# Hybrid encoder trunk on one core: every second expert-up tile as 512-column matmuls, and 112 of 256 router candidates

## What is computed

```python
def peer_ffn(h, w_query, q_norm_peer, sub_keys_1, sub_keys_2, expert_u, expert_v):
    s1, s2 = ...                      # 8 heads, 128 scores each, per token
    v1, i1 = lax.top_k(s1, 16)
    v2, i2 = lax.top_k(s2, 16)
    cand_s = v1[..., :, None] + v2[..., None, :]          # 16 x 16 = 256 sums
    cand_i = i1[..., :, None] * 128 + i2[..., None, :]
    top_s, top_pos = lax.top_k(cand_s, 16)                # of 256
    idx = jnp.take_along_axis(cand_i, top_pos, axis=-1)
    g = jax.nn.softmax(top_s, axis=-1)
    ...
    act = gelu(u[idx] . h)            # u: 16384 x 1024
    y = sum(g * act * v[idx])         # v: 16384 x 1024
```

## Time and profile before

| | us |
|---|---|
| median of three runs | 2226.91 (2225.76 to 2228.22) |
| the profiled execution, its own time | 2227.43 |
| its span, first to last instruction | 2225.6 |
| TensorE busy | 2164.8 (97%) |
| VectorE busy | 1656.9 (74%) |
| ScalarE busy | 1217.0 (55%) |

### The profile page before, as it was taken

How to read it: one execution, slowest core, us unless ns; L and a number is a source line. 1 busy time by engine, 2 the same in 40 slices (tenths; PEclk the granted TensorE clock), 3 DMA queues, 4 the chain that set the end, 5 groups by cost and what they waited for, 6 DMA issues and landing times.

```text
span 2225.6 us, 45150 instructions
## 1 busy us (share of the span) xinstructions
PE 2164.8 (97%) x14996; PEld 1996.6 (90%) x14996; DVE 1656.9 (74%) x3155; ACT 1217.0 (55%) x2134; POOL 268.7 (12%) x298
## 2 busy tenths in 40 slices
PE   4999999999999999999989999999999999999998
PEld 4889989999999988888878899899999999888887
DVE  6787766889589956777557868588895998567765
ACT  3656555444577654545455565644445776454544
POOL 0210000000157500000002100000001772000000
PEclk7999999999999999999999999999999999999999
DMA  8566655555533357787545666455555334588765
GB/s 321 169 209 216 209 171 169 180 180 178 185 127 114 114 195 255 253 257 229 196 174 171 224 213 214 138 182 183 180 184 174 114 113 135 195 274 256 254 214 162
DMA packets 114452, 427.48 MB, mean 192 GB/s; under 512 B 12704, under 2 KB 12960, under 8 KB 113056
## 3 DMA queue, kind: packets, MB, share of 16 engines
q1 hardware_dynamic: 114336, 426.08, 57.3%
HBM read 424.98 MB, written 1.05 MB: 191 GB/s over the span
## 4 chain that ended last, share of the span: by engine, by line
PE 94%; DVE 2%; issue 1%; DMA 1%; ACT 1%; POOL 0%; SPq 0%; ACTq 0%; DVEq 0%; POOLq 0%
PE pj L1290 18%; PE pj L1291 17%; PE pj L1292 17%; PE wk L1290 10%; PE wk L1292 10%; PE wk L1291 10%; PE wk L1602 5%; DMA arena<-in_front 1%; PE wk L1402 1%; PE wk L1379 1%; PE wk L1341 1%; PE wk L1395 1%; PE wk L1542 0%; PE wk L1315 0%; PE wk L1424 0%
## 5 line engine op out<-in xcount | busy, mean ns | idle before, releaser
L797 DVE TENSOR_TENSOR lo<-raw,hi 128x1024 fp32r<-128x1024 f32 x683 | 840.3, 1232 | 475.8 <-ACT hi L471 468.0
L471 ACT ACTIVATE hi<-raw 128x1024 fp32r<-128x1024 f32 x683 | 721.6, 1057 | 468.6 <-PE wk L1292 345.1
L1290 PE MATMUL pj<-mov_hi,hi 128*128 128x256 f32 x3248 | 945.5, 291 | 31.6 <-DVE mov_lo L848 27.5
L1291 PE MATMUL pj<-mov_lo,hi 128*128 128x256 f32 x3248 | 921.3, 284 | 0.0
L1292 PE MATMUL pj<-mov_hi,lo 128*128 128x256 f32 x3248 | 921.2, 284 | 0.0
L1290 PEld LDWEIGHTS pj<-mov_hi,hi 128*128 128x128 f32 x3248 | 624.2, 192 | 47.1 <-DVE mov_lo L848 30.4
L1291 PEld LDWEIGHTS pj<-mov_lo,hi 128*128 128x128 f32 x3248 | 625.9, 193 | 0.2
L1292 PEld LDWEIGHTS pj<-mov_hi,lo 128*128 128x128 f32 x3248 | 624.9, 192 | 0.0
L1290 PE MATMUL wk<-hi,mov_hi 128*128 128x512 f32 x1024 | 398.6, 389 | 1.7 <-DVE mov_lo L1239 1.7
L1292 PE MATMUL wk<-hi,mov_lo 128*128 128x512 f32 x1024 | 398.4, 389 | 0.0
L1291 PE MATMUL wk<-lo,mov_hi 128*128 128x512 f32 x1024 | 398.4, 389 | 0.0
(11 more groups left out here) (184 smaller groups left out, 1507.9 us busy)
## 6 DMA issues: line engine op xcount, KB each, us to landing
raw<-in_stream SPq DMA_DIRECT2D x684, 512.0 KB, 3.3
arena<-in_ada SPq DMA_DIRECT2D x72, 512.0 KB, 4.8
onehot_a<-in_ada SPq DMA_DIRECT2D x24, 512.0 KB, 4.6
arena<-in_front SPq DMA_DIRECT2D x4, 2048.0 KB, 19.3
arena<-in_taba SPq DMA_DIRECT2D x2, 1536.0 KB, 19.4
arena<-in_keys SPq DMA_DIRECT2D x2, 1024.0 KB, 6.3
x<-in_xT SPq DMA_DIRECT2D x1, 1024.0 KB, 5.0
arena<-in_mix SPq DMA_DIRECT2D x2, 512.0 KB, 16.1
```

What stands on the lines that cost most here:

```text
L471: nc.scalar.activation(hi[j % SPLIT][:, :], raw[j % RAW][:, :], ACT.Copy).then_inc(hi_done, 1)
L797: nc.vector.tensor_tensor(lo[j % SPLIT][:, :], raw[j % RAW][:, :], hi[j % SPLIT][:, :].bitcast(f32), ALU.subtract).then_inc(lo_done, 1)
L1290: pe.matmul(out, w_h, m_h, start=first, stop=False)
L1291: pe.matmul(out, w_h, m_l, start=False, stop=False)
```

## The change

**TensorE.** `mov_hi` and `mov_lo` of the first 8 chunks become one tensor `mov`, in which the high and the low part of a chunk lie side by side as 512 columns. The even ones of the 96 early up tiles use `project_half`: for each chunk one matmul of `hi` with all 512 columns (hi*hi in the left half of the bank, hi*lo in the right), and one of `lo` with the 256 high ones into the left half. The odd ones, the mixed tiles and all else go as before.

**ScalarE and VectorE.** For an even tile j, ScalarE copies the left half to `arena` (`early_half`), VectorE adds the right half to it (`second_half`, which frees the bank), and ScalarE takes the Gelu of it in place, before it evicts tile j+1. The adding of tile j stands in VectorE's order ahead of the `lo` of tile j+4, number j+1.

**The router.** `cand` has 112 places instead of 256: 4 times 16 (first half's places 0 to 3) and 12 times 4; the 16 largest sums of two sorted lists are always among these. Forming them takes two instructions, and each `max`, `match_replace` and `max_index` on it reads 112 values. The decode has five instructions more, with one `lo` subtraction more within it.

```diff
+CAND = 4 * 16 + 12 * 4
...
-        mov_hi = sb("mov_hi", [P, 12, SEQ], f32r)
-        mov_lo = sb("mov_lo", [P, 12, SEQ], f32r)
+        mov = sb("mov", [P, KC, 2, SEQ], f32r)
+        w_hi = sb("w_hi", [P, 4, SEQ], f32r)
+        w_lo = sb("w_lo", [P, 4, SEQ], f32r)
...
-        cand = part(256)
-        candr = part(256)
+        cand = part(CAND)
+        candr = part(CAND)
...
-                    act.wait_ge(tile_done, t + 1 + SPLIT)
-                    nc.scalar.activation(arena[:, bass.ds(i * 4 + j, 1), :].squeeze(1), pj[j % 2][:, 0:SEQ],
-                                         ACT.Gelu_apprx_tanh).then_inc(out_free, 1)
+                    if j % 2:
+                        wait_alone(act, out_free, l * OUTS + i * 4 + (O_PEER + j + 2))
+                        nc.scalar.activation(group(j - 1), group(j - 1), ACT.Gelu_apprx_tanh)
+                        act.wait_ge(tile_done, t + 1 + SPLIT)
+                        nc.scalar.activation(group(j), pj[1][:, 0:SEQ], ACT.Gelu_apprx_tanh).then_inc(out_free, 1)
+                    else:
+                        act.wait_ge(tile_done, t + 1 + SPLIT)
+                        nc.scalar.activation(group(j), pj[0][:, 0:SEQ], ACT.Copy).then_inc(early_half, 1)
...
+                def second_half(j):
+
+                    dve.wait_ge(early_half, l * (EARLY // 2) + j // 2 + 1)
+                    dve.wait_ge(out_free, l * OUTS + (O_PEER + j + 2))
+                    nc.vector.tensor_tensor(arena[:, j, :], arena[:, j, :], pj[0][:, SEQ:2 * SEQ], ALU.add)\
+                        .then_inc(out_free, 1)
+
                 def split_early(n):
                     for _ in range(min(n, EARLY - early[0])):
                         j = early[0]
+                        if j % 2:
+                            second_half(j - 1)
                         rest_of(L0 + (T_PEER + AHEAD + j), j + AHEAD)
                         early[0] += 1
...
-                nc.vector.tensor_scalar(pos_i[:, 0, :], tp, 4, None, ALU.logical_shift_right)
-                link(nc.vector.tensor_scalar(pos_i[:, 1, :], tp, 15, None, ALU.bitwise_and))
+                for n, (op, by) in enumerate(((ALU.logical_shift_right, 4), (ALU.logical_shift_right, 2),
+                                              (ALU.bitwise_and, 15), (ALU.bitwise_and, 12))):
+                    e = nc.vector.tensor_scalar(place_i[:, n, :], tp, by, None, op)
+                link(e)
+                split_early(1)
                 nc.vector.tensor_copy(sel_if, sel_i)
-                link(nc.vector.tensor_copy(pos_f, pos_i))
+                nc.vector.tensor_copy(place_f[:, 4, :], tp)
+                link(nc.vector.tensor_copy(place_f[:, 0:4, :], place_i))
+
+                nc.vector.scalar_tensor_tensor(pos_f[:, 0, :], place_f[:, 1, :], -12.0, place_f[:, 0, :], ALU.add, ALU.max)
+                link(nc.vector.scalar_tensor_tensor(place_f[:, 3, :], place_f[:, 4, :], 64.0, place_f[:, 3, :], ALU.is_ge,
+                                                    ALU.mult))
+                link(nc.vector.tensor_tensor(pos_f[:, 1, :], place_f[:, 2, :], place_f[:, 3, :], ALU.subtract))
                 split_early(1)
...
+                        wh, wl = chunk(j, k)
+                        both = mov[:, k, :, :].rearrange("p a s -> p (a s)")
+                        if k < KC - 1:
+                            pe.matmul(out, wh, both, start=k == 0, stop=False)
+                            pe.matmul(out[:, 0:SEQ], wl, mov_hi(k), start=False, stop=False)
+                        else:
+                            pe.matmul(out[:, 0:SEQ], wl, mov_hi(k), start=False, stop=False)
+                            last = pe.matmul(out, wh, both, start=False, stop=True)
+                    return last
```

More of the change, by code:

```diff
@@ L220, in trunk, with mov_of, mov_hi, mov_lo @@
         F_BANK = (2, 4, 3, 5)
+        def mov_of(side, k, n):
+            return mov[:, k:k + n, side, :] if k < KC else (w_hi, w_lo)[side][:, k - KC:k - KC + n, :]
+        def mov_hi(k):
+            return mov_of(0, k, 1).squeeze(1)
+        def mov_lo(k):
+            return mov_of(1, k, 1).squeeze(1)
         def y_pairs(br, i):
@@ L1329, in project, with project_half @@
                             between()
-                        last = product(pj[bank][:, 0:SEQ], *chunk(j, k), mov_hi[:, at[k], :], mov_lo[:, at[k], :],
+                        last = product(pj[bank][:, 0:SEQ], *chunk(j, k), mov_hi(at[k]), mov_lo(at[k]),
                                        k == 0, k == KC - 1)
+                    return last
+                def project_half(t, j, o, bank, chunks=None, between=None):
+                    pe.wait_ge(lo_done, t + 1)
+                    pe.wait_ge(out_free, l * OUTS + o + 1)
+                    out = pj[bank][:, :]
+                    for k in range(KC):
+                        if chunks is not None:
+                            pe.wait_ge(mov_ready, l * M_READY + (chunks + k + 1))
+                        if between is not None and k == KC // 2:
+                            between()
+                        wh, wl = chunk(j, k)
[6 more added lines that the diff above has]
+                            last = pe.matmul(out, wh, both, start=False, stop=True)
                     return last
@@ L1614, in _ @@
                                 tokens(i, j, 1)
-                            last = product(pj[j % 2][:, 0:SEQ], *chunk(j, k), mov_hi[:, k, :], mov_lo[:, k, :],
+                            last = product(pj[j % 2][:, 0:SEQ], *chunk(j, k), mov_hi(k), mov_lo(k),
                                            k == 0, k == KC - 1)
```

53 lines of the change are left out of this document (31 added, 22 removed).

## The result

The changed kernel takes **2240.23 us** (median of 4 runs, 2238.72 to 2243.03) against 2226.67 for the kernel before (median of 4): a ratio of 1.006, interval 1.0048 to 1.0073. It is 13.6 us slower. The forecast was +8.8 us with a range of 2225 to 2243: the direction and the range held, and the size fell short by 4.8 us. The profiled execution took 2240.32 us with a span of 2238.5, so between the two profiled executions the span grew by 12.9 us.

What follows compares the result with a forecast made beforehand. TensorE was taken to set the time. Picks and softmax place in two layers, less the joining gain, 2 x (7.0 + 2.5) - 10.2 = +8.8 us on 2227.43, gave 2236.2, median 2235.7 us; range 2225 to 2243.

Steps and rivals of the forecast that it cites:

- What bounds the kernel, and where: Early stage: TensorE's unbroken matmuls set the time; VectorE's additions come late in the picks and at the softmax place.
- The gain by joining: Even early tiles on TensorE: 13.3 ns saved for each of 768 joined matmuls, 10.2 us in all.
- The router: VectorE's router loop: the smaller list saves 0.86 us a round, 13.8 us a layer, none of it time gained.
- The tolerance and the picks: Additions may start 1.69 us late; VectorE's pick instructions delay tiles 62, 64, 66, 70, 74, costing 7.0 us per layer.
- The softmax place: Tile 80's addition waits behind softmax steps and a subtraction on VectorE, so tile 82 starts late: 2.5 us per layer.
- What is late next: nothing: Behind tile 82's late start nothing further is delayed: `lo` tiles are ahead and tile 84's gates are ready.
- Fewer late additions (17%): Rival, 17%: tiles 62 and 64 on time, picks stall about 4.4 us a layer: 2231, or 2227 with more lag absorbed.
- The picks without delay (10%): Rival, 10%: additions never late in the picks, only the softmax place costs: 2221.7, or 2216.7 if that is hidden.
- Stalls in the router loop (10%): Rival, 10%: slower additions (0.6 us) also stall TensorE in the router loop and lengthen picks: 2241 to 2244.
- a joined form that gains nothing (3%): Rival, 3%: a 512 behind a 256 keeps the whole cost of both, so the 10.2 us fall away: 2245.9.

Runs made afterwards that it cites:

- Removing the softmax place alone: Changed kernel with tile 80 copied and added ahead of the `lo` of tile 83 and the softmax steps: 2234.02 us, ratio 1.0029 to the kernel before.
- removing both: Changed kernel with tiles 60 to 79 multiplied and evicted as before the change, and tile 80 added ahead of the softmax steps: 2222.84 us, ratio 0.9975.
- the order by width: Changed kernel with each even tile's matmuls reordered: seven of 512 columns, eight of 256, one of 512: 2242.01 us, ratio 1.0063 to the kernel before.
- the fastest kernel: Changed kernel with tiles 60 to 79 as before, tile 80 added ahead of the softmax, joined tiles' matmuls grouped by width: 2219.54 us, ratio 0.9965.
- joining alone: Changed kernel with the old router (256 sums, old decode), keeping joined matmuls and additions: 2239.38 us, ratio 1.0052 to the kernel before.
- tiles 60 to 79 not joined: Changed kernel with tiles 60 to 79 multiplied and evicted as before the change, other even early tiles joined: 2231.81 us, ratio 1.0017 to the kernel before.
- the long late bank: Kernel before with three useless ScalarE copies at tile 80, holding its bank 2.3 us late: 2234.05 us, ratio 1.0028.
- the short late bank: Kernel before with one useless ScalarE copy at tile 80, holding its bank 1 us late: 2229.87 us, ratio 1.0011.

## Why the prediction was right in its direction and short in its size

**What bounds the kernel, and where: right.** TensorE sets the time; the stops stand where VectorE's queue is densest and at the softmax place, and nowhere else. Removing the softmax place alone gave back 6.2 to 6.9 us of 7.3 by medians and ratios, removing the picks alone 8.4 to 9.9 of 11.4, and removing both gave 17.4 of 18.7 (2240.23 to 2222.84), with no wait for an addition left.

**The gain by joining: the step that failed.** I took 13.3 ns for each joined matmul, "because both streams have a new weight load for every matmul and differ only in columns". It is 7 ns: 5.4 us instead of 10.2, and these 4.8 us are, by size, the whole error of the sum. The rates of the earlier trace rows are rates of streams of one width. In a stream that changes width twice in every chunk each change costs 2.5 ns more, as the order by width showed; that is 5 of the 6.3 ns, and the remaining 1.2 has no experiment. The prediction had noted that no row shows the two forms alternating, and should have kept the range open there instead of taking the upper end. The Trainium skill (TensorE: Matmul & The Clock Gate, Back-to-back issue gap) gives the gap of a matmul as its columns by the clock plus 2.5 ns, and gives this for an isolated one, not for a stream with a weight load before each, as this is; an estimate by that rule is 2.5 ns saved a joined pair. Measured are 7 in this order and 10.8 in the order by width (0.087 us over 8). So the rule gives too little in either order, and my 13.3 too much; the kernel as it was written lies somewhat nearer to the rule, the order by width nearer to the rates of this trace.

**The router: right.** A `max` on the list of 112 takes 272 ns, no stop appeared in the router loop, and in two comparisons (alone, and in the fastest kernel) the change is worth nothing that shows. In the third, the kernel after against joining alone, it adds 3.5 us of stops in the picks.

**The tolerance and the picks: right, 1.45 us too large over both layers.** Forecast were 0.5, 1.4, 1.6, 0, 1.5, 0 and 1.5 us for tiles 62 to 74 with 0.1 for each restart, 7.0 in all; measured 0.70, 1.29, 1.52, 0, 1.38, 0 and 1.39, 6.28. Part of the difference comes from the step that failed: a pair of tiles takes 5.70 us instead of 5.65, so that VectorE has 0.05 us more between additions at each pair. The idle time before subtraction 66 is 0.66 us where 0.8 was forecast. An addition takes 0.414 us on average, against 0.42, and whether it reads a bank (414 ns) or SBUF alone (418) makes no difference that shows:

```profile
L1111 DVE TENSOR_TENSOR arena<-arena,pj 128x256 f32<-128x256 f32 x96 | 39.8, 414 | 20.4 <-ACT arena L712 19.6 <-DVE arena L1199 0.4
...
L1154 DVE MAX8 arena<-arena 128x8 f32<-128x112 f32 x32 | 8.7, 272 | 0.0
```

(groups by line of the kernel after: busy us, mean ns, idle before and its releasers).

**The softmax place: right in its mechanism, short by the clock.** Forecast 2.5 us a layer; measured 2.46 in the second layer, and 3.98 in the first, where the clock fell. "What is late next: nothing" was true of the transfers and of the engines and not of TensorE's own rate. Over both layers that is 1.4 us.

**The sum.** -10.2 became -5.4 (+4.8), +14.0 became +12.55 (-1.45), +5.0 became +6.4 (+1.4): +4.75 us, which is the difference between +8.8 and +13.6. The middle term's error and the last one's cancel, so that the sum's whole error looks like the joining alone; that they do so is luck, as is the agreement to 0.1 us, since the measured difference has an interval of 10.7 to 16.3 us and this list of terms comes from one execution, whose span grew by 12.9.

**The rivals.** Fewer late additions (17%) didn't happen: both tiles 62 and 64 are late. The picks without delay (10%) is what "tiles 60 to 79 not joined" made by hand. Stalls in the router loop (10%) and a joined form that gains nothing (3%): neither. The time of 2240.23 us lies at the upper edge of the forecast's own range and only 1 us below the 2241 to 2244 of the stalling router loop, and has none of that rival's causes, which only the list of stops tells.

## What to carry to other kernels

When an engine with slack takes over the freeing of a buffer, its share of busy time says nothing; what counts is its longest unbroken stretch of queued work against the time the consumer can do without the buffer, and every place where that stretch is longer becomes a stop. Such places can be left out: the change applied to all tiles cost 13.6 us, and applied to all but tiles 60 to 79, with one addition moved ahead of the softmax, gained 5 to 8. A rate read from a uniform stream can be faster than what a mixed one gives, as here; where the order is free, put like widths together.

## What the runs showed of the hardware

**Mixed widths.** At full clock, matmuls of 512 columns follow after 226.7 ns and of 256 after 120.0 in streams of their own. Alternating, the two together take 353 ns instead of 346.7, and a pair of tiles with 16 changes of width takes 0.030 us more than one with 4.

**The clock after a short stop.** I had not expected that a stop of under 3 us in a busy stream could cost anything besides its length. At the softmax place, in the profiled executions of four kernels (after, joining alone, order by width, tiles 60 to 79 not joined), TensorE waited 2.65 to 2.69 us in each of two layers, and behind six of the eight stops the granted clock was at its half level for some microseconds (0.50 to 0.65 as the mean of stretches that partly reach beyond the fall), which cost about 1.5 us each time and once 2.8. Behind waits of 2.40 us (two, in the kernel before with the long late bank) and of 1.3 us or less (the picks and the short late bank) it stayed at 1.00, and so it did in the kernels where TensorE has no stop there. That the stop brings the fall is likely from these, and isn't shown: the kernel before was not run with a stop of 2.66 us at this place. Why two of the eight were spared stays open as well.

That a fall needs no joined matmul is shown, by the kernel before itself, ahead of its early stage. Timeline of TensorE and the stretch that follows:

```profile
306.27 0.70 PE L1315 MATMUL wk<-arena,const 128*128 128x256 f32 x2 [0.77 <-ACT arena L657]
309.57 0.39 PE L1290 MATMUL pj<-mov_hi,hi 128*128 128x256 f32 x1 [2.60 <-DVE mov_lo L848]
```
```profile
311.30:314.60 3.30, 3.30 (x13) 2.97 (x14) 3.12 (x9) 2.22 (x5) 0.00 (x0) 0.50 0.00 0
```

TensorE waits 0.77 us, does two matmuls, waits 2.60 us, and works at half the clock from 311.2 us on for over 3 us. All thirteen profiled executions have this wait (2.59 or 2.60 us) and a fall beside it, in both layers. It doesn't settle the softmax place, where the stop stands alone in a stream that is busy on both sides. How long the falls beside it last differs between executions, which may be one source of their spread.

**Time per value on VectorE.** From 256 to 128 values a `max` loses 1.08 ns a value. Carried on to 112 values that would give 266 ns, and 272 were measured.
